# Two transformer blocks on one core: reordered small steps between the first block's projection tiles

## The reference

```python
def first_block(...):
    a = rmsnorm(h, norm1[i])
    u, qf, kf, vf, fl, qs, ks_, vs = jnp.split(a @ w_in[i], IN_SPLITS, axis=-1)
    y_pool = multiscale_pool_mixer(u, pool_w[i], pool_scale[i])      # window means, 64x64 weights by group
    log_f = jax.nn.log_sigmoid(fl + forget_bias[i])
    y_fox = head_rmsnorm(forgetting_attention(qf, kf, vf, log_f), fox_out_gain[i], FOX_HEADS)
    y_sb = head_rmsnorm(stick_breaking_attention(qs, ks_, vs), sb_out_gain[i], SB_HEADS)
    h = h + jnp.concatenate([y_pool, y_fox, y_sb], axis=-1) @ w_out[i]
    a = rmsnorm(h, norm2[i])
    h = h + (jax.nn.silu(a @ w_gate[i]) * (a @ w_up[i])) @ w_down[i]
```

## Time and profile before

| what | value |
|---|---|
| three runs, median | 799.98 us (799.8 to 800.46) |
| profiled execution, its own span | 798.0 us, 12187 instructions |
| median of the runs above that span | 2.0 us |
| TensorE busy | 787.6 us (99%) |
| VectorE, ScalarE, GpSimd busy | 531.7, 429.6, 29.7 us |
| granted TensorE clock, mean over the span | 0.999 |

### The profile page before, as it was taken

The page is one execution under the profiler, slowest core; times in us unless marked ns, Lnnn a source line. Parts: engine busy times, 40 slices in busy tenths (PEclk is TensorE's granted clock), DMA queues, the critical chain, the costliest instruction groups (busy, mean ns, idle before and its releaser), DMA issues.

```text
span 798.0 us, 12187 instructions
## 1 busy us (share of the span) xinstructions
PE 787.6 (99%) x4716; PEld 693.5 (87%) x4716; DVE 531.7 (67%) x621; ACT 429.6 (54%) x565; POOL 29.7 (4%) x35
## 2 busy tenths in 40 slices
PE   8999999999999999999999999999999999999997
PEld 8989989888888888888888887999988888888885
DVE  7865557766666567866666566766977766666665
ACT  6556658454544548753544536565557644454444
POOL 0000100000000000000000000002420000000000
PEclk9999999999999999999999999999999999999999
DMA  8633333655545543665545554452444655554521
GB/s 332 238 118 126 123 115 138 224 186 183 209 167 203 187 181 113 237 234 181 209 165 204 187 181 159 148 195 106 159 178 152 225 210 177 191 197 172 209 105 53
DMA packets 20798, 141.16 MB, mean 177 GB/s; under 512 B 2449, under 2 KB 2705, under 8 KB 4385
## 3 DMA queue, kind: packets, MB, share of 16 engines
q1 hardware_dynamic: 20192, 138.65, 48.3%
q0 software_dynamic: 576, 2.10, 0.8%
HBM read 139.69 MB, written 1.05 MB: 176 GB/s over the span
## 4 chain that ended last, share of the span: by engine, by line
PE 95%; DVE 2%; ACT 2%; issue 1%; DMA 1%; SPq 0%; DVEq 0%; ACTq 0%
PE ps L1457 93%; ACT whi L679 1%; PE ps L1463 1%; DMA raw<-wstream 1%; DVE x L1206 0%; ACT squared L694 0%; DVE xa L1018 0%; PE ps L1694 0%; DVE wlo L1007 0%; PE ps L1664 0%; PE ps L1896 0%; DVE xg L1201 0%; DVEq L270 0%; ACT L912 0%; PE ps L1696 0%
## 5 line engine op out<-in xcount | busy, mean ns | idle before, releaser
L1457 PE MATMUL ps<-xa,whi 128*128 128x512 f32 (+2 forms) x1744 | 488.8, 348 | 0.0
L1457 PE MATMUL ps<-xa,wlo 128*128 128x256 f32 (+1 forms) x1376 | 383.1, 282 | 0.0
L1007 DVE TENSOR_TENSOR wlo<-raw,whi 128x2048 fp32r<-128x2048 f32 x128 | 293.1, 2290 | 83.8 <-ACT whi L679 83.6
L1457 PEld LDWEIGHTS ps<-xa,whi 128*128 128x128 f32 x1744 | 302.5, 188 | 44.6 <-issue 2.1
L1457 PEld LDWEIGHTS ps<-xa,wlo 128*128 128x128 f32 x1376 | 258.7, 189 | 1.1
L679 ACT ACTIVATE whi<-raw 128x2048 fp32r<-128x2048 f32 x128 | 244.2, 1908 | 7.0 <-PE ps L1457 6.8
L1457 PE MATMUL ps<-whi,hhi 128*128 128x512 f32 x240 | 93.8, 391 | 0.0
L1457 PE MATMUL ps<-whi,hlo 128*128 128x512 f32 x240 | 93.7, 390 | 0.0
L1457 PE MATMUL ps<-wlo,hhi 128*128 128x512 f32 x240 | 93.5, 390 | 0.0
L873 ACT ACTIVATE hhi<-arena 128x512 fp32r<-128x512 f32 x30 | 19.0, 633 | 89.0 <-PE ps L1457 82.5
L859 ACT ACTIVATE arena<-ps 128x512 f32<-128x512 f32 x33 | 19.7, 596 | 87.5 <-PE ps L1457 87.3
(11 more groups left out here) (216 smaller groups left out, 531.3 us busy)
## 6 DMA issues: line engine op xcount, KB each, us to landing
raw<-wstream SPq DMA_DIRECT2D x128, 1024.0 KB, 4.8
gain_row<-rows_in POOLq DMA_DIRECT2D x4, 512.0 KB, 3.8
x<-x_in SPq DMA_DIRECT2D x2, 512.0 KB, 4.0
raw<-wstream SPq DMA_DIRECT2D x2, 512.0 KB, 5.5
out<-x SPq DMA_DIRECT2D x4, 256.0 KB, 2.1
xg<-const_in SPq DMA_DIRECT2D x1, 912.0 KB, 11.7
small<-small_in SPq DMA_DIRECT2D x1, 152.0 KB, 6.0
arena<-meta_in SPq DMA_DIRECT2D x1, 64.0 KB, 4.6
```

Of the source, the lines that this page charges most:

```text
L1007: nc.vector.tensor_tensor(wlo[slot][:], raw[slot][:], whi[slot][:].bitcast(F32), ALU.subtract).then_inc(lo_ready, 1)
L1457: return nc.tensor.matmul(o, lhsT, rhs, start=start, stop=stop, skip_group_check=True)
```

## The change

Four kinds of edits, all in the first stage. (1) In `fox_turn` all six full transposes come first and the four small ones behind them. (2) `fox_apply` of pair j moves from slots 9, 11, 13 to 10, 12, 14, and its rank from 2 to 4.5, so it stands behind the next pair's scores (or behind `sb_score`, or `sb_later`); `sb_apply` moves from 16, 18, 22 to 17, 19, 22. (3) `fox_norm` moves from 10, 13, 15 to 12, 14, 16, `sb_norm` from 18, 20, 24 to 19, 21, 24. (4) `pool` moves from slot 7 to 8, the first `values` from 5 to 6.

```diff
-    after[7].append(("pool", 0))
-    for n, s in enumerate((5, 9, 11, 14, 17, 19)):
+    after[8].append(("pool", 0))
+    for n, s in enumerate((6, 9, 11, 14, 17, 19)):
         after[s].append(("values", n))
     for j in range(PAIRS):
-        after[(10, 13, 15)[j]].append(("fox_norm", j))
-        after[(18, 20, 24)[j]].append(("sb_norm", j))
+        after[(12, 14, 16)[j]].append(("fox_norm", j))
+        after[(19, 21, 24)[j]].append(("sb_norm", j))
...
-        after[(9, 11, 13)[j]].append(("fox_apply", j))
+        after[(10, 12, 14)[j]].append(("fox_apply", j))
...
-        after[(16, 18, 22)[j]].append(("sb_apply", j))
+        after[(17, 19, 22)[j]].append(("sb_apply", j))
...
-            "fox_apply": 2, "sb_apply": 2, "fox_turn": 3, ...
+            "fox_apply": 4.5, "sb_apply": 2, "fox_turn": 3, ...
...
                     for h in range(2):
                         for n, c in enumerate((0, 144, 144 + P)):
                             nc.tensor.transpose(ps[:, 2 + h, n * 160:n * 160 + P], soft[:, h, c:c + P], ident[:])
+                    for h in range(2):
                         for n, c in enumerate((144 + 2 * P, P)):
                             ins = nc.tensor.transpose(ps[0:META, 2 + h, n * 160 + P:(n + 1) * 160], soft[last, h, c:c + META], ident[last, last])
                         ins.then_inc(fox_turned, 1)
```

More of the change, by code:

```diff
@@ L162, in schedule_first @@
         after[(14, 17, 21)[j]].append(("sb_later", j))
-        after[(16, 18, 22)[j]].append(("sb_apply", j))
+        after[(17, 19, 22)[j]].append(("sb_apply", j))
     rank = {"gates": 0, "forget_sums": 0, "values": 2, "pool": 5, "fox_norm": 1, "sb_norm": 1, "fox_rows": 1, "sb_mask": 1,
-            "fox_apply": 2, "sb_apply": 2, "fox_turn": 3, "sb_later": 3, "fox_scale": 3, "sb_plus": 5, "fox_score": 4, "sb_score": 4}
+            "fox_apply": 4.5, "sb_apply": 2, "fox_turn": 3, "sb_later": 3, "fox_scale": 3, "sb_plus": 5, "fox_score": 4, "sb_score": 4}
     return [st for s, slot in enumerate(slots)
```

## The result

| | before | after |
|---|---|---|
| median of 19 runs each | 800.14 us (799.75 to 801.74) | 801.51 us (801.04 to 803.19) |
| ratio | | 1.0019, 95% interval 1.0012 to 1.0025 |
| profiled execution, span | 798.0 us | 799.3 us |

The changed kernel is 1.37 us slower, inside the range, a little above the forecast of 801.1.

The account below looks back on a forecast made before the run. TensorE, busy 99% of the span, was taken to bound the kernel. Gains of 1.78 us against waits of 2.91 made it 1.13 us longer than the 799.98 us median: 801.1 us, range 800.0 to 802.2.

Parts of the forecast that it names:

- The turns: Full transposes together, then the small ones, in `fox_turn`: 0.24 us saved per turn, 0.72 for three (lower end 0.45).
- Four merged neighbours: Part-array products put beside scores at four places: one entering and one leaving saved, 0.20 us each, 0.80 (0 to 1.60).
- the dear: Rival: scores-to-products step costs a full return, the four places save nothing; 1.93 us longer, 801.9; chance 16%.
- the free direct change: Rival: scores-to-products step costs nothing, 0.40 us saved at each place; 0.33 us longer, 800.3; chance 10%.
- The first norm's wait: First `fox_norm`, two slots behind its products: the wait for GpSimd's low part of the squares goes, 0.26 us gained.
- Wait (a): Before the first turn: without the pool products as cover, TensorE waits 0.57 us for VectorE's scaled softmax.
- Wait (c): Second stick-breaking scores, slot 15: the norm that lay in their gap moves to slot 16, costing 0.24 us.
- Wait (d): First `sb_apply`, slot 17: waits 1.69 us (1.4 to 2.0) for the third `fox_norm`'s VectorE step behind a weight split.
- Wait (b): Fourth `values`, slot 14: waits 0.41 us (0 to 0.9) for VectorE's copy of tile 13, behind ScalarE's later copies.
- TensorE's side: Fourth `values`: TensorE's own work meanwhile, tile 13, tile 14 and a norm, 6.22 us.
- The other side: Fourth `values`: the ScalarE and VectorE path from the end of the products to `values`, 6.63 us.
- 5.82 from the softplus to the end of the copy: Fourth `values`: stretch from ScalarE's softplus to the end of VectorE's copy of tile 13, 5.82 us of the 6.63.

## Why the prediction was right, and which term was off

*The turns* (0.72): 0.69 by the run, and 53.25 to 54.21 = 0.96 us in the profile, where the kernel before takes 1.20 from 44.07 to the scores, in TensorE's timeline:

```profile
45.27 0.97 PE L1457 MATMUL ps<-arena 64*128 64x144 f32 x8
```

Right; but alone in the kernel before they gain nothing, which the sum didn't need and I had not seen.

*Four merged neighbours* (0.80). Scores take 0.90 us (44.28 to 45.18), products with the values 0.95, both behind one another 54.21 to 56.06 = 1.85: the direct step costs as much as the one change that stood there anyway, and one entering and one leaving disappear. Neither the dear nor the free direct change came. By the Trainium skill, "TensorEngine Tiling (Array Packing)", Key Properties, a change of the tiling mode drains TensorE; the trace agrees in that the direct step, too, costs about one change. The three places undone in one kernel gave 0.15, 0.15 and 0.21, the first two against a place that is itself 0.05 cheaper than the old one. The fourth, the pool products behind the scores, was not undone by itself.

*The first norm's wait* (0.26): 62.34 to 62.58 is 0.24 us, where the earlier trace rows had a wait in it. Right.

*Wait (a)* 0.57: 0.60 by the distances, 0.58 by the run. *Wait (c)* 0.24: 0.24. *Wait (d)* 1.69: 1.70. Right, and the last of them is 1.7 of the 2 us between the changed kernel and the one with the norm in slot 15.

*Wait (b)* 0.41: **0.66, the term that was mis-sized.** TensorE's side was right: from the end of the products (65.86) to where the `values` could start (71.82 + 0.24) 6.20 us, predicted 6.22. The other side was to be 6.63 and took 72.72 - 65.86 = 6.86. The step that failed is "5.82 from the softplus to the end of the copy", read from a place where GpSimd did nothing beside line 1189 (its steps there start at 63.73 and 72.37). In the changed kernel it is 6.10 (66.47 to 72.14 + 0.43), because line 1189 takes 0.90 instead of 0.59. VectorE in the kernel before, then ScalarE, VectorE and GpSimd in the changed one:

```profile
70.91 0.59 DVE L1189 TENSOR_SCALAR sb_parts<-arena 128x832 fp32r<-128x832 f32 x1
```

```profile
66.47 0.84 ACT L841 ACTIVATE arena<-ps 128x832 f32<-128x832 f32 x1
...
70.26 0.90 DVE L1189 TENSOR_SCALAR sb_parts<-arena 128x832 fp32r<-128x832 f32 x1
...
72.14 0.43 DVE L1136 COPY arena<-ps 128x272 f32<-128x272 f32 x1
...
69.97 0.74 POOL L647 TENSOR_TENSOR ya<-ysq,ya 128x256 fp32r<-128x256 f32 x1 [8.03 <-ACT ya L838]
```

The moved products moved their squares too, and with them GpSimd's step: I had counted its order and its slack, not what runs beside it.

The sum with these: waits 3.20, gains 0.72 + 0.80 + 0.26 = 1.78, so 1.42; the medians give 1.37. Of the 0.4 us between forecast and median 0.25 is wait (b), and 0.16 that 19 runs put the kernel before at 800.14, not 799.98. The prediction took a loss of 1.1 us as too small to be told from none; with 19 runs each the interval of the ratio (1.0012 to 1.0025) leaves out 1.

## What to carry to other kernels

A step that is moved on the bound engine moves in every in-order queue: before moving it, list what it will stand behind on each engine and who waits for it there; here one norm behind one weight split cost as much as all the gains together, and was cured by one changed number. A gain on the bound engine counts only up to the next wait, so a small edit is measured with those waits away, not alone in a kernel that has them. Price a wait from start to start, and look at what will run beside a moved step, not only ahead of and behind it.

## What the runs showed of the hardware

**VectorE beside GpSimd.** Line 1189 takes 0.59 us alone and 0.90 beside line 647; line 1149, four instructions, takes 1.04 alone and 1.36 beside it (63.72 in the kernel with the norm in slot 11, whose line 647 runs from 63.50 for 0.74). The other way round the kernel before has a line 647 of 2.66 us beside the split at 86.56, where its others take 0.73 to 0.92 (spans on GpSimd are rough in this profile):

```profile
86.78 2.66 POOL L647 TENSOR_TENSOR ya<-ysq,ya 128x256 fp32r<-128x256 f32 x1 [13.62 <-ACT ya L838]
```

By the Trainium skill, "GPSIMD Engine Reference", 1. Specifications, GpSimd shares its SBUF interfaces with VectorE, with contention for VectorE instructions that run in a two-port mode or have two SBUF inputs. The trace agrees, in both directions; the split has two such inputs, `raw` and `whi`, and in which mode lines 1189 and 1149 ran no row shows.

**A fall of the clock behind a stop, in one trace.** In the kernel with one neighbour undone TensorE stops for the same 1.64 us in slot 17. The granted clock is still full from the end of the stop (89.20) to 91.00; from there to 94.00 it is 0.52, nearly all of it at the lower of the two levels (1.2 instead of 2.4 GHz). The windows of its trace (stretch, length, then each engine's busy time, PEclk, DMA share, GB/s) and its timeline:

```profile
89.20:91.00 1.80, 1.80 (x19) 1.68 (x19) 0.94 (x3) 0.76 (x2) 0.00 (x0) 1.00 0.65 137
91.00:94.00 3.00, 3.00 (x15) 2.97 (x14) 0.00 (x0) 1.48 (x3) 0.73 (x1) 0.52 0.66 273
```

```profile
89.20 0.97 PE L1457 MATMUL ps<-arena 128*64 128x256 f32 x12 [1.64 <-DVE ytmp L1046]
...
99.42 0.40 PE L1457 MATMUL ps<-ya,exact 128*128 128x256 f32 x2
```

The same stretch of the changed kernel's profiled execution has the full clock behind the same stop:

```profile
91.00:94.00 3.00, 3.00 (x26) 3.00 (x25) 0.00 (x0) 2.35 (x2) 0.55 (x1) 1.00 0.58 240
```

From the start of `sb_apply` to the norm behind tile 18 this execution takes 89.20 to 99.42 = 10.22 us, the changed kernel 88.90 to 97.57 = 8.67: the fall costs 1.55 us. It is the only one ahead of 790 us in the 14 traces of this case. Five of these have the stop, and four of the five keep the full clock behind it, so that the stop brings the fall is not shown. The prediction had no term for it.
